# Half of the transposes of a chunked scan on TensorE: products with the identity, or the transpose form

## What is computed

```python
def step(s, inp):
    r_t, w_t, k_t, v_t, kk_t, a_t = inp
    sa = jnp.einsum('bhvk,bhk->bhv', s, -kk_t)
    s = (s * w_t[:, :, None, :] + sa[..., None] * (kk_t * a_t)[:, :, None, :]
         + v_t[..., None] * k_t[:, :, None, :])
    return s, jnp.einsum('bhvk,bhk->bhv', s, r_t)
```

## Time and profile before

| | us |
|---|---|
| median of 3 runs | 3560.22 |
| lowest and highest of them | 3550.71, 3563.6 |
| profiled execution, its own time | 3554.39 |
| span of its instructions | 3552.7 |

### The profile page before, as it was taken

One profiled execution on the slowest core, in us unless ns is written; L12 is line 12 of the kernel. 1 busy time (PEld: TensorE's weight loads), 2 busy tenths in 40 slices (PEclk: granted clock), 3 DMA queues, 4 the chain that ended last, 5 costly groups with the idle time before them and its releaser, 6 DMA issues.

```text
span 3552.7 us, 155850 instructions
## 1 busy us (share of the span) xinstructions
PE 3312.4 (93%) x72354; PEld 2871.3 (81%) x72354; DVE 2133.6 (60%) x3890; ACT 765.1 (22%) x1815; POOL 388.7 (11%) x536
## 2 busy tenths in 40 slices
PE   7989899898999999299999999999999999999998
PEld 3575767767455545299999999999999999999997
DVE  4566667575344434666666666666666666666665
ACT  3434344444244443000000000000000000000002
POOL 0141524334211000000000000000000000000001
PEclk9999999999999999699999999999999999999999
DMA  8200000000311113399898898999889989898996
GB/s 358 73 5 9 18 10 17 5 20 5 99 33 33 44 54 107 128 325 286 284 290 278 290 285 281 286 291 287 283 287 288 284 282 292 284 289 287 283 288 211
DMA packets 570775, 671.20 MB, mean 189 GB/s; under 512 B 56942, under 2 KB 463750, under 8 KB 567054
## 3 DMA queue, kind: packets, MB, share of 16 engines
q1 hardware_dynamic: 564430, 641.85, 55.5%
q0 software_dynamic: 5520, 19.34, 2.4%
q10 hardware_dynamic: 176, 0.05, 0.0%
HBM read 631.68 MB, written 28.30 MB: 186 GB/s over the span
## 4 chain that ended last, share of the span: by engine, by line
PE 56%; issue 1%; SPq 1%; DVE 0%; DMA 0%; ACT 0%; DVEq 0%
PE banks L2515 34%; PE banks L2540 21%; PE banks L2456 2%; SPq L2363 1%; SPq L2370 0%; DMA e_wgu<-in_e_up 0%; DVE e_wgu L2819 0%; SPq L2373 0%; DVE e_wgu L2888 0%; DVE e_xe L2877 0%; DVE e_wsum L2717 0%; ACT e_xp L2655 0%; ACT e_xT L2655 0%; DVE e_wgu L2722 0%; DVE e_hid L2769 0%
## 5 line engine op out<-in xcount | busy, mean ns | idle before, releaser
L2540 PE MATMUL banks<-e_hid,e_wd 128*64 128x144 f32 x11264 | 1242.0, 287 | 6.7 <-issue 3.8
L2540 PEld LDWEIGHTS banks<-e_hid,e_wd 128*64 128x64 f32 x11264 | 744.4, 137 | 8.3 <-issue 8.2
L2515 PE MATMUL banks<-e_xsum,e_wsum 128*64 128x72 f32 x11264 | 514.3, 226 | 10.5 <-issue 7.8
L2515 PE MATMUL banks<-e_xT,e_wgu 128*64 128x72 f32 x11264 | 511.7, 226 | 12.6 <-issue 10.3
L2515 PE MATMUL banks<-e_xsum,e_wgu 128*64 128x72 f32 x11264 | 510.9, 226 | 7.9 <-issue 7.8
L2515 PEld LDWEIGHTS banks<-e_xsum,e_wsum 128*64 128x64 f32 x11264 | 492.7, 137 | 13.8 <-issue 11.0
L2515 PEld LDWEIGHTS banks<-e_xT,e_wgu 128*64 128x64 f32 x11264 | 491.4, 137 | 15.1 <-issue 14.8
L2515 PEld LDWEIGHTS banks<-e_xsum,e_wgu 128*64 128x64 f32 x11264 | 489.5, 137 | 10.1 <-issue 10.0
L2750 DVE TENSOR_TENSOR e_gu<-e_first,banks 128x288 f32<-128x288 f32 x176 | 79.9, 454 | 673.7 <-ACT e_first L2636 515.6
L2636 ACT ACTIVATE e_first<-banks 128x144 f32<-128x144 f32 x176 | 51.3, 291 | 1414.2 <-PE banks L2515 1414.2
L2515 PE MATMUL banks<-e_xT,e_wsum 128*64 128x72 f32 x5632 | 252.8, 226 | 2.8 <-issue 2.7
(11 more groups left out here) (401 smaller groups left out, 4754.3 us busy)
## 6 DMA issues: line engine op xcount, KB each, us to landing
e_wgu<-in_e_gate SPq DMA_DIRECT2D x704, 256.0 KB
e_wgu<-in_e_up SPq DMA_DIRECT2D x704, 256.0 KB
e_wd<-in_e_down SPq DMA_DIRECT2D x704, 256.0 KB, 4.0
h_wmod<-in_w_mod SPq DMA_DIRECT2D x24, 1024.0 KB, 16.5
wblk<-in_w_in SPq DMA_DIRECT2D x22, 512.0 KB, 21.6
h_x<-in_x_sample SPq DMA_DIRECT2D x8, 512.0 KB, 7.0
wo<-in_w_out SPq DMA_DIRECT2D x2, 2048.0 KB, 12.0
scratch_ffn<-hT_x SPq DMA_DIRECT2D x8, 512.0 KB, 5.2
```

The lines of the kernel that those rows point to most:

```text
L2515: last = nc.tensor.matmul(bank[4 + 2 * (n % 2) + g][c, q * HT:(q + 1) * HT], a[:, k, c], b[:, k, :], start=(k == 0), stop=(k == HALF - 1))
L2540: last = nc.tensor.matmul(bank[k // PER_BANK][c, at:at + TOK], wd[n % WD][:, b, k * P + h * CH:k * P + (h + 1) * CH], hid[n % 2][:, b, :], ...
```

## The change

A local helper `turned` takes the place of the product in the three transposing helpers. Where the output's rows start at partition 0 it issues `nc.tensor.transpose(out, src, ident)`, elsewhere the product as before. Operands, order, semaphores and all other engines stay as they are.

```diff
+                    def turned(out, rows, src, ident):
+
+                        if rows.start == 0:
+                            return nc.tensor.transpose(out, src, ident)
+                        return nc.tensor.matmul(out, src, ident, start=True, stop=True)
+
@@ v_major
-                                        last = nc.tensor.matmul(bank[banks[d]][FAR[d][h], n * HN:(n + 1) * HN],
-                                                                v[HS[h], c * CH:(c + 1) * CH], K.idc[HS[h], :],
-                                                                start=True, stop=True)
+                                        last = turned(bank[banks[d]][FAR[d][h], n * HN:(n + 1) * HN], FAR[d][h],
+                                                      v[HS[h], c * CH:(c + 1) * CH], K.idc[HS[h], :])
@@ tok_major
-                                        last = nc.tensor.matmul(bank[d][FAR[d][h], n * CH:(n + 1) * CH],
-                                                                src[HS[h], piece(d, 2 * g + i)], K.idc[HS[h], :],
-                                                                start=True, stop=True)
+                                        last = turned(bank[d][FAR[d][h], n * CH:(n + 1) * CH], FAR[d][h],
+                                                      src[HS[h], piece(d, 2 * g + i)], K.idc[HS[h], :])
@@ inverse_start
-                                    last = nc.tensor.matmul(bank[5][f, at:at + CH],
-                                                            W0[f, i, :] if d else TW[g % 2][f, d, 1, i, :],
-                                                            K.idc[f, :], start=True, stop=True)
+                                    last = turned(bank[5][f, at:at + CH], f,
+                                                  W0[f, i, :] if d else TW[g % 2][f, d, 1, i, :], K.idc[f, :])
```

## The result

| | before | after |
|---|---|---|
| median, us | 3555.5 (4 runs) | 3663.6 (4 runs) |
| span of the profiled execution, us | 3552.7 | 3664.8 |
| TensorE matmuls, busy us | 3312.4 | 3449.2 |

What follows compares the result with a forecast made beforehand. It took the scan as bound by a chain passing between engines, paced on TensorE by each block's last instruction. Block savings near 0 and mixing at 0 summed to -1 us, giving a 3559 us median; range 3548 to 3594 us.

Steps and rivals of the forecast that it cites:

- I take 0 because the full-array rows show no stop: Scan blocks: mixing transposes and products costs 0 us, read from full-array rows; -8.5 to +34 us for the unknown.
- the missing row: Scan quarters: no profile row shows a transpose in one quarter beside a product in another; cost of mixing unknown.
- rival B: Scan blocks: array drained at each change of kind, 160 ns each, 109 us in all, 3690 to 3703 us; chance 0.04.
- A: Scan blocks: transposes don't share the array with products in other quarters, +15 to +34 us, 3575 to 3594 us; chance 0.17.
- The cover of `tok_major`: tok_major: VectorE releases the next level within 0.05 us of the block's end, 1.8 us over 36 blocks.
- A longer block would be on the path nearly at once: tok_major: only 0.05 us a block covers a slowdown before it delays what follows.
- the transpose form takes one step of its quarter in place of two: Scan quarters: a 64-column transpose costs about 55 ns, one step, in place of a product's two of 59 ns.
- the blocks' ends are set by the quarters that keep their products: All three scan blocks: relieved quarters stand beside unchanged chains that end last, so the saving is about 0.
- Rival D, the clock: Scan stretches: transposes hold the clock less well, so some run at 1.2 GHz; 10 us, 3570 us; chance 0.04.

Runs made afterwards that it cites:

- e8: Kernel before with two of inverse_start's eight products as transposes, both in one quarter; the next kind starts 0.15 to 0.16 us later; no whole time given.
- e11: Changed kernel plus two warming products in TensorE's wait for T0 in 32 rounds; 1.0257 times the kernel before, against 1.0301 for the changed kernel.
- e1: Transposes kept only in tok_major, products in v_major and inverse_start as in the kernel before; 1.0055 times the kernel before, +20 us.
- e4: Changed kernel with transposes batched ahead of products, 1 / 1 / 5 changes inside tok_major / inverse_start / v_major; 1.0026 times the kernel before.
- e2: Transposes kept only in inverse_start, products in v_major and tok_major as in the kernel before; 1.0110 times the kernel before, +39 us.
- e3: Transposes kept only in v_major, products in tok_major and inverse_start as in the kernel before; 1.0108 times the kernel before, +38 us.
- e12: Kernel before plus identity product-transpose-product series in TensorE's T0 wait; changes take 0.10 to 0.11 us at whole array, 0.20 us at 64 columns; no whole time given.
- e6: Kernel before, no transpose form, with three unused whole-array products ahead of each tok_major; 1.0086 times the kernel before, +31 us.
- e9: As e4 with batches of half the size, 3 / 3 / 17 changes inside tok_major / inverse_start / v_major; 1.0073 times the kernel before.
- e7: e2 plus two warming products in TensorE's wait for T0 in 32 rounds; 1.0098 times the kernel before, where e2 took 1.0110.

## Why the prediction was wrong

**The step that failed** is "I take 0 because the full-array rows show no stop". It carried the price of a change of kind from products over the whole array, where it is free, to products in quarters, where it costs 88 to 114 ns over the ordinary step (the change, e8). Everything else in the sum hung on it. I had named the missing row, priced it as rival B and then left B outside the range at a chance of 0.04. The rows had no transpose next to a product of 64 columns, so they weren't evidence enough to go that low, and the trace did have a price for leaving the whole array: 0.20 us between the warming products and `v_major`. The range, with its end at A's 3594 us, was wrong for the same reason.

**Rival B's mechanism** is what happens. Its 109 us for the drains looks like the 108 measured, but that is luck. B counted 7 changes in `inverse_start`, and called it alternating; the order there is transpose, product, transpose, two products, transpose, product, transpose, which is 6 changes, and (36 x 14 + 4 x 36) x 0.16 = 104 us. Its sizes: 160 ns more at each change was taken from the length of a MATMUL. Measured, a transpose-to-product change starts 172 ns after, where a step is 59, so 114 more; product to transpose 149, so 91 more; and the first step behind a change is 107 ns, 49 more. A group with two changes and a step costs 320 ns more (0.437 us in place of 0.117), where B with A came to 380 to 440. B also left out the stalls, the low clock and the changes at the ends of a block.

**The account.** Of the 112 us between the two profiled executions 107 lie in the scans. By place: the `v_major` blocks grew from 8 to 38 us, 30 more; the four first rounds (from one `inverse_start` to the next) from 45 to 65 us, 20 more; the 28 rounds behind them from 361 to 413 us, 52 more; the ends of the scans 6 more. These are readings. By cause there is only an estimate. Inner rounds with neither a stall nor a low clock take 14.0 to 14.15 us after (10 of them) and 11.4 before, where there is one alone; that is about 2.7 us for each of 36 groups, 96 us. It is more than the 1.23 + 0.99 us inside the blocks, since a block is also entered and left by a change. `v_major` adds 4 x 5.8 = 23 us at the full clock. The stalls give back 27 us (30.9 to 3.9). The low clock adds the 16 us of e11 or more, 27 us by the third of a microsecond that a group loses. That makes 108 to 119 us, against 107: right in size, and no proof of each term.

**The cover of `tok_major`.** "A longer block would be on the path nearly at once" was right for VectorE's wait, but missed the stalls of TensorE: half of e1's cost was given back outside the block.

**Right** was that the transpose form takes one step of its quarter in place of two (e4's rows). That the blocks' ends are set by the quarters that keep their products, so that nothing was to be won even without the emptying, stays an argument from the order; no run has a block that mixes the kinds for free.

**Rival D, the clock**, is there as a follower. The page that I cited, "TensorE: Matmul & The Clock Gate", Part 4 of the Trainium skill, says that transposes don't count as activity as products do. Here e1 runs 288 of them in its scans and e4 576, and they spend 0 and 7 us of them at the low clock; the kernel before, without any, has one low stretch of 7 us. So here the number of transposes doesn't bring the clock down. The change, e2 and e3 have it low for 85, 75 and 38 us, but e1, whose blocks empty TensorE no less often, for none; why the clock fell in those three and not in e1, no run shows.

## What to carry to other kernels

Before a transpose form replaces products with the identity, look at the products that stand beside it. Beside fp32 products over the whole array it came for nothing, even with 64 columns of its own. Beside products of 64 columns each change of kind cost TensorE about 90 to 115 ns over the ordinary step, and the two kinds never ran side by side. If both kinds must be mixed there, issue all of one kind and then all of the other: e4 is 1.0026 times the time before, the change 1.0301, with the same instructions. And a price read at one tile shape is no evidence for another: where no row has the pair in question, the drained pipeline belongs inside the range.

## What the runs showed of the hardware

- Next to fp32 products of 64 columns, a change between transpose and product empties TensorE: 146 to 172 ns from start to start in quarters for a step of 58, 0.20 us for a step of 0.11 in 128 by 64 tiles. Next to products over the whole array it is free, at 128 by 128 (e12) and for the 32 transposes of 128 by 64 in the kernel before.
- A change of tile shape between products costs as much: 205 ns from 128 by 128 to 64 by 64 (before), 148 ns back (e12).
- Transposes in two quarters that read different halves and write the same one start together (e4), as products in different quarters do. No run had them in any others.
- The fp32 transpose takes one step of its quarter, 0.05 to 0.06 us, and the product two.
- Some 31 us of the kernel before are stalls of TensorE in the scans that no semaphore ends. They shrink to 3 to 8 us when blocks in each round take longer (e1, e4, e6, e9, the change), so a slowdown of up to that can be nearly free, once. e3, with a longer block only once a pair, keeps 27 us of them.
- The low clock lost a third of a microsecond of each in the mixed blocks (0.65 for 0.44 us a group). Half is the most that the two levels allow. What it costs a scan is known only roughly: 16 us for 34 in e11 (2 to 29), and in e7 4 us for 44 (from -13 to 22).
